# The last spreading of a decoder layer: identity products around the last down product, and the sampled tile in four quarters of the partitions

## The chip, the cores and the metric

One NeuronCore of a Trainium2 chip runs the whole kernel in one launch. The metric is the device time in microseconds, here the median of a few plain executions. A further execution is recorded by the hardware profiler; every row below comes from it. Engines that matter here: TensorE (matmul, PE in the rows, its weight loads PEld), VectorE (DVE), ScalarE (ACT), GpSimd (POOL) and SyncE (SP), which issues most of the transfers.

## The reference, cut to what matters

A decoder layer for 512 prompt tokens and 32 sampled tokens (8 sequences of 4), rows of 1024 float32. The change concerns only the last lines: the weighted outputs of the experts are added to the residual rows, and the result goes through a final RMS norm.

```
y = jnp.zeros((n, D_MODEL), jnp.float32)
for e in range(N_EXPERTS):
    h = jax.nn.silu(xt @ w_gate[e]) * (xt @ w_up[e])
    y = y + combine[:, e:e + 1] * (h @ w_down[e]).astype(jnp.float32)
...
xp = xp + _hier_moe(...)
xs = xs + _hier_moe(...)
y_prompt = _rms(xp, final_norm_g)
y_sample = _rms(xs, final_norm_g)

def _rms(x, g):
    y = xf * lax.rsqrt(jnp.mean(xf * xf, axis=-1, keepdims=True) + EPS)
    return (y * g.astype(jnp.float32)).astype(x.dtype)
```

## The kernel before, in words

The order of the work is written out by hand in the source, engine by engine; semaphores connect them. The 544 tokens lie in five tiles of rows: tiles 0 to 3 of 128 prompt tokens, and tile 4 (`PT`) of the 32 sampled ones.

The 16 experts are worked off in a row of turns. A turn gathers the tokens of an expert, transposes them, multiplies by the gate and up weights (`first_of`), and after the product of the two the down weights (`last_of`). The output rows, scaled by their weights (`y_out`: half the columns by ScalarE, half by VectorE), are added to the residual rows in DRAM (`scratch_x3`) by an indirect DMA of GpSimd. So it goes for the first 14 turns. The last two (`E - 2` and `E - 1`, 64 places each) leave their 64 + 64 output rows in the tile `y_last` instead (it lies in `tabs`). TensorE then spreads them over the tokens: `rows_of_last` (in `cst`) holds for each of the 128 rows a one in the column of its token, and a product of it with `y_last` gives for a tile of tokens what the last two experts add. The sums of a tile lie in the PSUM banks `SUM_BANK[i] + n`, tile i and column half n.

For the light last expert the hidden rows are first transposed (`light_turned`, line 1295, `ps<-cst,qT`), copied by VectorE (L2569) and then multiplied with the down weights (`light_down`, `ps<-ring,qT 64x512`, the weights in four pieces with a semaphore each, `wd_last0` to `wd_last3`).

Meanwhile SyncE loads the residual rows back from `scratch_x3` into `x2` (in `xr`) once all adds have landed (`y_all`), tile 0 first. It issues them on the same queue as the weights. Tile 4 waits besides for the product that still reads this place.

How a tile gets its sum differs. For tiles 0, 1 and 4 the product goes to PSUM and VectorE adds it to `x2` (`summed`). For tiles 2 and 3 TensorE does the adding: an identity product (`ident` with `x2`, `ps<-xr,cst` in the rows) opens the accumulation and the spreading product closes it. Then ScalarE squares and sums a tile's rows and takes the root (`square_and_root`), VectorE takes the reciprocal and multiplies by it and by the weights of the norm (`last_norm`, `gf`), and SyncE stores. The order of the spreading is `SPREAD`, that of the norms `NORM_ORDER` (0, 1, 2, 4, 3). All this stands in one side of a branch on `more`, which is zero here; the other side serves overflowing experts.

Of the kernel before, what the change touches and what calls it, by code (L numbers as in the profile page):

```python
# [21 lines left out]
ALU = mybir.AluOpType  # L22
ACT = mybir.ActivationFunctionType
AX = mybir.AxisListType.X
# [153 lines left out]
def hybrid_layer(nc, t, o):  # L178
# [5 lines left out]
    with ExitStack() as ctx:  # L184
# [156 lines left out]
        SPREAD = ((0, 0), (0, 1), (1, 0), (1, 1), (4, 0), (4, 1), (2, 0), (2, 1), (3, 0), (3, 1))  # L341
# [4 lines left out]
        gf = [buf[:, PT * W:TILES * W] for buf in (ugr, vnr)]  # L346
        y_last = tabs[:, 1024:2048]
# [117 lines left out]
        def _(sp):  # L465
# [206 lines left out]
            for i in range(TILES):  # L672
                if i == PT:
                    sp.wait_ge(sem("y_mm"), 2 * E - 2)
                load(x2[0:ROWS[i], i, :], scratch_x3[i * P:i * P + ROWS[i], :], "x3_in%d" % min(i, 3))
            for i in NORM_ORDER[0:TILES - 1]:
                sp.wait_ge(sem("out_ready"), NORMED[i] + 1)
                dst = o[0][i * P:(i + 1) * P, :] if i < PT else o[1]
                sp.dma_start(dst, x2[0:ROWS[i], i, :]).then_inc(sem("stored"), 16)
# [4 lines left out]
            sp.wait_ge(sem("stored"), 16 * (TILES + 1))  # L684
# [3 lines left out]
        def _(te):  # L688
# [771 lines left out]
            def last_expert_spread(i, n):  # L1460

                j = SUMMED[i][n] - 1
                te.wait_ge(sem("last_rows"), 2)
                te.wait_ge(sem("y_out%d" % n), E)
                bank = pb[SUM_BANK[i] + n]
                if i == PT:
                    te.wait_ge(sem("x3_summed"), SUMMED[0][n])
                    for q in (2 * n, 2 * n + 1):
                        ins = mm(bank[NS * (q % 2):NS * (q % 2) + NS, 0:256], rows_of_last[:, SEQ:TOK],
                                 y_last[:, 256 * q:256 * q + 256])  # L1470
                elif i in (2, 3):
                    te.wait_ge(sem("x3_in%d" % i), 16 if i < 3 else 32)
                    mm(bank, ident, x2[:, i, W * n:W * n + W], True, False)
                    ins = mm(bank, rows_of_last[:, P * i:P * i + P], y_last[:, W * n:W * n + W], False, True)
                else:
                    ins = mm(bank, rows_of_last[:, P * i:P * i + P], y_last[:, W * n:W * n + W])
                ins.then_inc(sem("spread_mm"), 1)

            def last_experts_spread():

                for i, n in SPREAD:
                    last_expert_spread(i, n)

            with te.If(more == 0):
                last_experts_spread()
            with te.Else():
                te.wait_ge(sem("y_out0"), E)
# [11 lines left out]
                last_experts_spread()  # L1499
# [3 lines left out]
        def _(act):  # L1503
# [369 lines left out]
            def squares_and_roots():  # L1873
# [3 lines left out]
                def square_and_root(i):  # L1877
                    if i in (2, 3):
                        act.wait_ge(sem("spread_mm"), SUMMED[i][1])
                        A(ring[:, 2 + i // 4, D * (i % 4):D * (i % 4) + D].rearrange("p (n w) -> p n w", n=2),  # L1880
                          ps[:, SUM_BANK[i]:SUM_BANK[i] + 2, :], ACT.Square,
                          accum_out=small[:, 2 * i:2 * i + 1]).then_inc(sem("x3_sq"), 1)
                    else:
                        act.wait_ge(sem("x3_summed"), SUMMED[i][1] if i < 2 else 6)
                        A(ring[0:ROWS[i], 2 + i // 4, D * (i % 4):D * (i % 4) + D], x2[0:ROWS[i], i, :], ACT.Square,
                          accum_out=small[0:ROWS[i], 2 * i:2 * i + 1]).then_inc(sem("x3_sq"), 1)
                    act.wait_ge(sem("x3_sq"), NORMED[i] + 1)
                    A(small[:, 32 + i:33 + i], small[:, 2 * i:2 * i + 1], ACT.Sqrt, bias=small[:, 16:17], scale=1.0 / D
                      ).then_inc(sem("rstd"), 1)

                for i in NORM_ORDER:
                    square_and_root(i)
# [13 lines left out]
        def _(dve):  # L1906
# [732 lines left out]
            def summed(i, n):  # L2639

                j = SUMMED[i][n]
                if n == 0:
                    dve.wait_ge(sem("x3_in%d" % min(i, 3)), 16 if i < 3 else 32)
                dve.wait_ge(sem("spread_mm"), j)
                bank = pb[SUM_BANK[i] + n]
                if i == PT:
                    for q in (2 * n, 2 * n + 1):
                        v = x2[0:NS, PT, 256 * q:256 * q + 256]
                        ins = V.tensor_tensor(v, bank[NS * (q % 2):NS * (q % 2) + NS, 0:256], v, ALU.add)
# [5 lines left out]
            def last_norm(i):  # L2655
                rows = ROWS[i]
                dve.wait_ge(sem("rstd"), 5 + TILES + NORMED[i])
                rs = small[0:rows, 32 + i:33 + i]
                link(V.reciprocal(small[:, 32 + i:33 + i], small[:, 32 + i:33 + i]))
                if i in (2, 3):  # L2660
                    for n in range(2):
                        ins = V.scalar_tensor_tensor(out=x2[:, i, W * n:W * n + W], in0=pb[SUM_BANK[i] + n], scalar=rs,
                                                     in1=gf[n], op0=ALU.mult, op1=ALU.mult)
                        if i == 3 or n == 1:
                            ins.then_inc(sem("out_ready"), 1)
                else:
                    for n in range(2):
                        v = x2[0:rows, i, W * n:W * n + W]
                        ins = V.scalar_tensor_tensor(out=v, in0=v, scalar=rs, in1=gf[n][0:rows, :],
# [3 lines left out]
            def sums_and_norms():  # L2673
# [3 lines left out]
                link(V.memset(small[:, 16:17], EPS))  # L2677
                summed(0, 0)
# [5 lines left out]
                summed(4, 1)  # L2684
# [230 lines left out]
```

## Time and profile before

| what | us |
|---|---|
| median of 3 plain executions | 715.03 (714.4 to 716.43) |
| profiled execution, its own time | 718.91 |
| its span in the trace | 717.2 |
| TensorE busy | 663.7 (93% of the span) |
| the last 17.4 us: from the first spreading product to the end | 699.8 to 717.2 |

Times in the rows are microseconds from the span's start, unless marked ns. A line number is that of the kernel before; L690 is the helper of nearly all products, so a product is told by its tiles: `ps<-tabs,cst` is a spreading product, `ps<-xr,cst` an identity product, `ps<-ring,qT` a down product. A float32 product is two passes on TensorE, so 16 instructions are 8 products. Instructions of one kind that follow each other are merged in a row with their count. The order lists below are of the program, not of an execution, and hold no times.

### The profile page before, as it was taken

Reading aid. Unit: us, or ns where it says so; the run is one execution under the profiler, and the core shown is the slowest. Engines: PE = TensorE matmul, PEld = TensorE weight load, DVE = VectorE, ACT = ScalarE, POOL = GpSimd, SP = SyncE. Lnnn points to the kernel's source line nnn. Section 1 sums busy time; section 2 is a strip of 40 time slices with the busy share of each in tenths; the row PEclk is TensorE's granted clock in tenths of the full one; section 3 lists DMA queues with packets and bytes.
Section 4 is the critical chain, followed back from the end, with each engine's and each line's share of the span. In section 5 each row is a group of like instructions: output and inputs, shape, how many; then the busy total and the mean of one; then the engine's idle time right before and its main releaser. Section 6 shows DMA issues by size and latency. Waiting matters only on the chain.

```text
span 717.2 us, 14789 instructions
## 1 busy us (share of the span) xinstructions
PE 663.7 (93%) x5458; PEld 427.2 (60%) x5458; DVE 260.9 (36%) x817; ACT 184.2 (26%) x460; POOL 143.8 (20%) x227
## 2 busy tenths in 40 slices
PE   4999998999998888989999977999999999889796
PEld 2486597847646356557555555865685856455342
DVE  4147210137435656765234582112111011111116
ACT  3110213112132883576332211011111010101104
POOL 0405017130143086500000202011211111110000
PEclk9999999999999999999999977999999999999999
DMA  9996138153479075602497258999999999999973
GB/s 336 377 341 210 49 134 291 45 191 118 149 236 358 31 219 154 215 1 83 158 429 301 83 177 291 405 382 392 377 372 408 370 384 386 372 390 390 357 256 131
DMA packets 56785, 185.60 MB, mean 259 GB/s; under 512 B 9021, under 2 KB 30814, under 8 KB 50562
## 3 DMA queue, kind: packets, MB, share of 16 engines
q1 hardware_dynamic: 44914, 152.54, 56.2%
q0 software_dynamic: 11792, 32.05, 14.6%
q8 instruction: 45, 0.74, 0.4%
q14 instruction: 34, 0.28, 0.1%
HBM read 172.57 MB, written 13.93 MB: 260 GB/s over the span
## 4 chain that ended last, share of the span: by engine, by line
PE 75%; DMA 10%; DVE 6%; SPq 4%; ACT 2%; issue 2%; DVEq 0%; POOLq 0%; ACTq 0%
PE ps L690 69%; DMA ring<-in_w_down_dram 6%; SPq L467 3%; PE ps L939 2%; DMA ring<-in_cmp_pages_dram 1%; PE ps L1209 1%; DMA ring<-in_w_in_dram 1%; SPq L427 1%; DMA h_rows<-tabs 1%; PE ps L786 1%; PE ps L966 1%; ACT tabs L1650 1%; DMA ugr<-h_rows,qbd 1%; DVE vnr L2200 0%; DVE xr L2196 0%
## 5 line engine op out<-in xcount | busy, mean ns | idle before, releaser
L690 PE MATMUL ps<-ring,xr 128*128 128x512 f32 (+3 forms) x640 | 140.0, 415 | 9.6 <-DMA ring<-in_w_in_dram 9.6
L690 PEld LDWEIGHTS ps<-ring,xr 128*128 128x128 f32 (+1 forms) x640 | 68.8, 152 | 72.9 <-issue 59.8
L690 PE MATMUL ps<-ring,vnr 128*32 128x128 f32 (+1 forms) x1152 | 78.9, 326 | 2.8 <-DMA ring<-in_w_gate_dram 2.3
L690 PE MATMUL ps<-ring,work 128*32 128x128 f32 (+2 forms) x512 | 70.7, 368 | 0.5 <-DVE xr L2317 0.5
L690 PEld LDWEIGHTS ps<-ring,vnr 128*32 128x32 f32 (+1 forms) x1152 | 54.9, 124 | 27.0 <-issue 10.9
L427 POOL DMA_DIRECT2D ring<-in_sel_pages_dram x96 | 51.6, 537 | 92.1 <-issue 57.1
L690 PE MATMUL ps<-ring 128*128 128x128 f32 (+1 forms) x512 | 60.2, 279 | 1.9 <-DMA ring<-in_cmp_pages_dram 1.9
L2821 POOL DMA_INDIRECT x_rows<-kvn,qbd x14 | 20.5, 1466 | 199.9 <-DVE kvn L2589 58.4
L690 PEld LDWEIGHTS ps<-ring 128*128 128x128 f32 x512 | 59.1, 191 | 2.4 <-DMA ring<-in_cmp_pages_dram 2.1
L2539 DVE COPY vnr<-ps 128x256 f32<-128x256 f32 (+3 forms) x16 | 8.1, 508 | 143.7 <-PE ps L1209 143.7
L690 PE MATMUL ps<-ring,qT 128*32 128x256 f32 (+2 forms) x320 | 52.8, 490 | 5.2 <-DMA ring<-in_w_down_dram 4.5
L427 POOL DMA_DIRECT2D ring<-in_cmp_pages_dram x64 | 34.8, 544 | 81.1 <-PE ps L690 54.3
L690 PEld LDWEIGHTS ps<-ring,work 128*32 128x32 f32 (+1 forms) x512 | 33.9, 130 | 28.4 <-issue 27.1
L1650 ACT ACTIVATE tabs<-tabs,rt 128x128 f32<-128x128 f32 (+3 forms) x64 | 35.4, 559 | 18.6 <-DVE rt L2053 18.6
L690 PEld LDWEIGHTS ps<-ring,qT 128*32 128x32 f32 (+2 forms) x320 | 19.9, 128 | 31.8 <-issue 28.0
L2053 DVE CUSTOM_DVE_ANT_0 tabs<-ps,tabs 128x128 f32<-128x128 f32 (+3 forms) x64 | 28.0, 487 | 14.7 <-PE ps L690 13.9
L1813 ACT COPY vnr<-ps 128x256 f32<-128x256 f32 (+3 forms) x16 | 7.0, 440 | 86.3 <-PE ps L1209 86.3
L939 PEld LDWEIGHTS ps<-cst,tabs 128*128 128x128 f32 x160 | 17.7, 144 | 12.1 <-issue 7.2
L939 PE MATMUL ps<-cst,tabs 128*128 128x128 f32 x160 | 22.7, 284 | 1.8 <-ACT xr L1660 0.9
L690 PE MATMUL ps<-xr,kvn 128*64 128x128 f32 (+2 forms) x264 | 22.9, 310 | 0.3 <-DVE xr L2156 0.3
L690 PE MATMUL ps<-vnr,ring 128*128 128x128 f32 x192 | 21.8, 275 | 0.0
L690 PEld LDWEIGHTS ps<-vnr,ring 128*128 128x128 f32 x192 | 21.6, 192 | 0.0
(401 smaller groups left out, 819.9 us busy)
## 6 DMA issues: line engine op xcount, KB each, us to landing
ring<-in_w_gate_dram SPq DMA_DIRECT2D x11, 2048.0 KB, 26.1
ring<-in_w_down_dram SPq DMA_DIRECT2D x10, 2048.0 KB, 33.5
ring<-in_w_up_dram SPq DMA_DIRECT2D x9, 2048.0 KB, 27.4
xr<-in_w_gate_dram SPq DMA_DIRECT2D x5, 2048.0 KB, 32.6
tabs<-in_w_up_dram SPq DMA_DIRECT2D x5, 2048.0 KB, 35.5
ring<-in_cmp_pages_dram SPq DMA_DIRECT2D x64, 128.0 KB, 5.1
ring<-in_cmp_pages_dram POOLq DMA_DIRECT2D x64, 128.0 KB, 5.3
ring<-in_w_in_dram SPq DMA_DIRECT2D x3, 2048.0 KB, 9.0
```

The costliest lines, as they stand in the source:

```text
L427: eng.dma_start(dst[:, 256 * j + part.start:256 * j + part.stop], table[bass.ds(page, 1), :, part].rearrange("o p n -> (o p) n")).then_inc ...
L467: sp.dma_start(dst, src).then_inc(sem(name), 16)
L690: return nc.tensor.matmul(out, lhsT, rhs, start=start, stop=stop)
L786: ins = nc.tensor.transpose(bank[:, 128 * m:128 * m + rows], src, ident[0:rows, 0:rows])
L939: ins = nc.tensor.transpose(pb[4 + g][:, at:at + P], prob[s % 3][:, g, n * k + P * m:n * k + P * m + P], ident)
L966: ins = nc.tensor.transpose(pb[7][:, P * h:P * h + P], oT[pair % 2][:, P * h:P * h + P], ident)
L1209: ins = nc.tensor.transpose(pb[k // 4][:, P * (k % 4):P * (k % 4) + cap], xe[par][0:cap, P * k:P * k + P], ident[0:cap, 0:cap])
L1650: A(v, v, ACT.Exp, scale=-1.0, bias=rt[:, 160 + u % 32:161 + u % 32], accum_out=rt[:, total:total + 1]).then_inc(sem("probs"), 1)
L1813: nc.scalar.copy(xeT[par][:, 0:4, 0:cap], pb[0][:, :].rearrange("p (k n) -> p k n", k=4)[:, :, 0:cap]).then_inc(sem("xt_ready"), 1)
L2053: return V.tensor_tensor_reduce(out, a, b, scale, 3.0e38, ALU.add, ALU.min, acc)
L2539: V.tensor_copy(xeT[par][:, 4:8, 0:cap], pb[1][:, :].rearrange("p (k n) -> p k n", k=4)[:, :, 0:cap]).then_inc(sem("xt_ready"), 1)
L2821: po.indirect_dma_start(scratch_x3, bass.IndirectOffsetOnAxis(slot_tokens[0:cap, n:n + 1].bitcast(U32), 0), ye[n % 2][0:cap, :], None, com ...
```

## The change

Four things change, all behind the last gate and up products.

TensorE: the branch on `more` is taken before the last expert's transposes. On the usual side the identity product of tile 2's first half (`own_rows(2, 0)`) stands between the transposes and the last down product, that of its second half (`own_rows(2, 1)`) behind the down product, ahead of the scaled copies. The two spreading products of tile 2 then stand alone.

The rows of tile 2 are the first that SyncE loads.

The sampled tile lies in four quarters of the partitions: 256 of its 1024 columns on each 32 partitions (`pt_quarters`), and the norm's weights in the same way (`gf_quarters`). SyncE loads and stores it in four pieces and the norm's weights in four more. One group of four products fills it, one VectorE instruction sums it, one norms it. ScalarE squares it before tile 2.

Each row's squares are then spread over four partitions. VectorE builds a matrix with ones where two partitions hold the same token (`same_row`), and TensorE multiplies it with the partial sums (128x1, `ps<-small,xr`), between the two halves of tile 3. ScalarE takes that root from PSUM.

On TensorE, at the end of the last gate and up products and around the last down product (`ps<-ring,qT`), before:

```order
L690 MATMUL ps<-ring,vnr 64x256 x7
L1295 MATMUL ps<-cst,qT 128x128 [waits y_out1,y_out0,hl_ready]
L1295 MATMUL ps<-cst,qT 128x128
L1457 TENSOR_LOAD ints
L1457 ISA x2
L690 MATMUL ps<-ring,qT 64x512 [waits y_out1,wd_last0,y_out0,h_ready]
L690 MATMUL ps<-ring,qT 64x512
L690 MATMUL ps<-ring,qT 64x512 [waits wd_last1]
```

And now:

```order
L701 MATMUL ps<-ring,vnr 64x256 x7
L1467 TENSOR_LOAD ints
L1467 ISA x2
L1504 COMPARE_AND_BRANCH
L1306 MATMUL ps<-cst,qT 128x128 [waits y_out1,y_out0,hl_ready]
L1306 MATMUL ps<-cst,qT 128x128
L701 MATMUL ps<-xr,cst 128x512 [waits y_out0,x3_in2]
L701 MATMUL ps<-ring,qT 64x512 [waits y_out1,wd_last0,y_out0,h_ready]
L701 MATMUL ps<-ring,qT 64x512
L701 MATMUL ps<-ring,qT 64x512 [waits wd_last1]
```

The read of the flag and the branch moved ahead of the transposes, and a product that waits for the load of tile 2 (`x3_in2`) stands ahead of the down product. Then the spreading from tile 1's second half on, before:

```order
L690 MATMUL ps<-tabs,cst 128x512 [waits y_out1,last_rows]
L690 MATMUL ps<-tabs,cst 32x256 [waits x3_summed,y_out0,last_rows]
L690 MATMUL ps<-tabs,cst 32x256
L690 MATMUL ps<-tabs,cst 32x256 [waits x3_summed,y_out1,last_rows]
L690 MATMUL ps<-tabs,cst 32x256
L690 MATMUL ps<-xr,cst 128x512 [waits x3_in2,y_out0,last_rows]
L690 MATMUL ps<-tabs,cst 128x512
L690 MATMUL ps<-xr,cst 128x512 [waits x3_in2,y_out1,last_rows]
L690 MATMUL ps<-tabs,cst 128x512
```

And now, to the end of tile 3:

```order
L701 MATMUL ps<-tabs,cst 128x512 [waits y_out1,last_rows]
L701 MATMUL ps<-tabs,cst 32x256 [waits y_out1,x3_summed,y_out0,last_rows]
L701 MATMUL ps<-tabs,cst 32x256 x3
L701 MATMUL ps<-tabs,cst 128x512 [waits y_out0,last_rows]
L701 MATMUL ps<-tabs,cst 128x512 [waits y_out1,last_rows]
L701 MATMUL ps<-xr,cst 128x512 [waits x3_in3,y_out0,last_rows]
L701 MATMUL ps<-tabs,cst 128x512
L701 MATMUL ps<-small,xr 128x1 [waits x3_sq,x3_summed,last_rows]
L701 MATMUL ps<-xr,cst 128x512 [waits x3_in3,y_out1,last_rows]
L701 MATMUL ps<-tabs,cst 128x512
```

Tile 2 has lost its identity products here, the four products of the sampled tile stand in one group, and the one-column product is new; it waits for ScalarE's square of the sampled tile.

The diff, cut to its core:

```diff
-        SPREAD = ((0, 0), (0, 1), (1, 0), (1, 1), (4, 0), (4, 1), (2, 0), (2, 1), (3, 0), (3, 1))
+        SPREAD = ((0, 0), (0, 1), (1, 0), (1, 1), (4, 0), (2, 0), (2, 1), (3, 0), (4, 1), (3, 1))
+        pt_quarters = x2[:, PT, 0:256]
+        gf_quarters = x2[:, PT, 256:512]
+        same_row = x2[:, PT, 512:512 + P]
+        SQUARED = (0, 1, PT, 2, 3)
...
-            for i in range(TILES):
-                if i == PT:
-                    sp.wait_ge(sem("y_mm"), 2 * E - 2)
-                load(x2[0:ROWS[i], i, :], scratch_x3[i * P:i * P + ROWS[i], :], "x3_in%d" % min(i, 3))
+            for i in (2, 0, 1, 3):
+                load(x2[:, i, :], scratch_x3[i * P:i * P + P, :], "x3_in%d" % i)
+            sp.wait_ge(sem("y_mm"), 2 * E - 2)
+            for q in range(4):
+                at = slice(256 * q, 256 * q + 256)
+                load(pt_quarters[NS * q:NS * q + NS, :], scratch_x3[SEQ:TOK, at], "vectors_in")
+                load(gf_quarters[NS * q:NS * q + NS, :], t["gf"][:, at].to_broadcast([NS, 256]), "vectors_in")
...
+                if i == PT:
+                    for q in range(4):
+                        sp.dma_start(o[1][:, 256 * q:256 * q + 256], pt_quarters[NS * q:NS * q + NS, :]).then_inc(sem("stored"), 16)
...
-            light_turned(E - 1)
             more = te.value_load(ints[0:1, 80:81], min_val=0, max_val=1)
-            last_of(E - 1)
+            def own_rows(i, n):
+                te.wait_ge(sem("x3_in%d" % i), 16)
+                te.wait_ge(sem("y_out%d" % n), E - 1)
+                mm(pb[SUM_BANK[i] + n], ident, x2[:, i, W * n:W * n + W], True, False)
...
+                if i == PT and n == 1:
+                    te.wait_ge(sem("x3_summed"), 5)
+                    te.wait_ge(sem("x3_sq"), SQUARED.index(PT) + 1)
+                    mm(pb[SUM_BANK[0] + 1][:, 0:1], same_row, small[:, 2 * PT:2 * PT + 1]).then_inc(sem("spread_mm"), 1)
+                    return
...
             with te.If(more == 0):
-                last_experts_spread()
+                light_turned(E - 1)
+                own_rows(2, 0)
+                last_of(E - 1)
+                own_rows(2, 1)
+                last_experts_spread(2)
...
+                elif i == PT:
+                    V.scalar_tensor_tensor(out=pt_quarters, in0=pt_quarters, scalar=rs, in1=gf_quarters,
+                                           op0=ALU.mult, op1=ALU.mult).then_inc(sem("out_ready"), 1)
...
+                link(V.tensor_reduce(four_units, ident.rearrange("p (q m) -> p m q", q=4), AX, ALU.add))
+                link(V.tensor_copy(same_row.rearrange("p (q m) -> p q m", q=4), four_units[:, None, :].to_broadcast([P, 4, NS])))
```

## Rows read from the trace of the kernel before

**Rows 1.** The chain that ended last, from 671 us: start, us, what.

```profile
681.48 12.28 PE ps L690 x80
...
694.26 0.45 PE ps L1295 x2
...
694.73 0.43 DVE qT L2569
...
699.01 0.67 ACT tabs L1853
...
699.82 11.74 PE ps L690 x32
...
711.58 1.12 ACT ring L1880 x2
...
712.73 0.31 ACT small L1888
...
713.06 0.17 DVE small L2659
...
713.93 0.74 DVE xr L2662
```

**Rows 2.** Line L683, the last two stores: issue to landing.

```profile
DMA to landing us min/median/max: 2.1/2.1/2.2
```

**Rows 3.** Timeline of PE, 671 to 700: start, us; in brackets idle before.

```profile
673.62 5.52 PE L690 MATMUL ps<-ring,qT 128*64 128x512 f32 x48 [2.09 <-DMA ring<-in_w_down_dram]
...
681.48 2.71 PE L690 MATMUL ps<-work,qT 128*64 128x512 f32 x8 [1.97 <-DVE qT L2569]
...
695.34 3.65 PE L690 MATMUL ps<-ring,qT 128*64 128x512 f32 x16 [0.64 <-DVE qT L2569]
```

**Rows 4.** Timeline of SyncE: the last weight piece, then the five residual loads.

```profile
672.37 0.91 SPq L467 DMA_DIRECT2D ring<-in_w_down_dram  x1
...
690.54 3.02 SPq L467 DMA_DIRECT2D xr<-x_rows  x5
```

**Rows 5.** DMA issues from 672.35 and from 690.5, landing last; then spacing (ns).

```profile
ring<-in_w_down_dram SPq DMA_DIRECT2D x1, 512.0 KB, 23.2
...
xr<-x_rows SPq DMA_DIRECT2D x1, 512.0 KB, 6.3
...
L467 SPq DMA_DIRECT2D xr<-x_rows x5: 338/424/1211, 690.5 to 693.1; - x5
```

**Rows 6.** Stretches: length, PE busy (instructions), granted clock, DMA share, GB/s.

```profile
672.00:676.00 4.00, 2.38 (x12) 1.00 1.02 402
679.10:682.50 3.40, 1.43 (x12) 1.00 0.76 319
682.50:685.90 3.40, 3.40 (x12) 0.50 0.74 278
693.80:695.30 1.50, 0.44 (x2) 1.00 1.05 421
```

**Rows 7.** Timeline of the tail, 699 to 707, VectorE and TensorE.

```profile
701.06 1.45 DVE L2652 TENSOR_TENSOR xr<-ps,xr 128x512 f32<-128x512 f32 x2 [1.11 <-PE ps L690]
...
703.42 0.58 PEld L690 LDWEIGHTS ps<-tabs,cst 128*32 128x32 f32 x8 [0.76 <-issue]
...
704.17 0.84 DVE L2649 TENSOR_TENSOR xr<-ps,xr 32x256 f32<-32x256 f32 x2
...
704.41 1.13 PE L690 MATMUL ps<-xr,cst 128*128 128x512 f32 x2
...
705.38 1.02 PE L690 MATMUL ps<-tabs,cst 128*128 128x512 f32 x2
...
706.23 1.02 PE L690 MATMUL ps<-xr,cst 128*128 128x512 f32 x2
```

**Rows 8.** Groups by shape: count, busy us, mean ns, idle before.

```profile
L690 PE MATMUL ps<-ring,qT 128*32 128x256 f32 x160 | 9.7, 382 | 0.0
L690 PE MATMUL ps<-small,ugr 128*128 128x1 f32 x8 | 0.9, 240 | 0.0
```

More of the change, by code:

```diff
@@ L1463, in last_expert_spread @@
                 te.wait_ge(sem("last_rows"), 2)
-                te.wait_ge(sem("y_out%d" % n), E)
+                if i == PT and n == 1:
[3 more added lines that the diff above has]
+                    return
+                for half in range(2):
+                    if i == PT or n == half:
+                        te.wait_ge(sem("y_out%d" % half), E)
@@ L1882, in square_and_root, with root @@
                           accum_out=small[:, 2 * i:2 * i + 1]).then_inc(sem("x3_sq"), 1)
-                    else:
[L1884 to L1892, printed above, removed]
+                    elif i == PT:
+                        act.wait_ge(sem("x3_summed"), 5)
+                        A(ring[:, 3, 0:256], pt_quarters, ACT.Square, accum_out=small[:, 2 * i:2 * i + 1]
+                          ).then_inc(sem("x3_sq"), 1)
+                    else:
+                        act.wait_ge(sem("x3_summed"), SUMMED[i][1])
+                        A(ring[:, 2, D * i:D * i + D], x2[:, i, :], ACT.Square,
+                          accum_out=small[:, 2 * i:2 * i + 1]).then_inc(sem("x3_sq"), 1)
+                def root(i):
+                    act.wait_ge(sem("x3_sq"), SQUARED.index(i) + 1)
+                    if i == PT:
+                        act.wait_ge(sem("spread_mm"), SUMMED[PT][1])
+                    A(small[:, 32 + i:33 + i], pb[SUM_BANK[0] + 1][:, 0:1] if i == PT else small[:, 2 * i:2 * i + 1], ACT.Sqrt,
+                      bias=small[:, 16:17], scale=1.0 / D).then_inc(sem("rstd"), 1)
+                square(0)
+                root(0)
+                square(1)
+                root(1)
+                square(PT)
+                square(2)
+                root(2)
+                root(PT)
+                square(3)
+                root(3)
             with act.If(more == 0):
@@ L2655, in last_norm @@
             def last_norm(i):
-                rows = ROWS[i]
                 dve.wait_ge(sem("rstd"), 5 + TILES + NORMED[i])
-                rs = small[0:rows, 32 + i:33 + i]
+                rs = small[:, 32 + i:33 + i]
                 link(V.reciprocal(small[:, 32 + i:33 + i], small[:, 32 + i:33 + i]))
@@ L2683, in sums_and_norms @@
                 last_norm(0)
-                summed(4, 1)
                 last_norm(1)
```

48 lines of the change are left out of this document (25 added, 23 removed).

## The prediction

> **What bounds the kernel now.** I read the last 45 us backwards, since the change touches nothing earlier. First the chain of waits in order of time [rows 1]. The last stretch has three parts. TensorE runs expert by expert (to 693.76), then a short relay with VectorE for the last expert: transposes at 694.26, copy of the hidden rows at 694.73, down product at 695.34. Then come the scaled copies (699.01) and, without a hole, 11.74 us of spreading products (699.82 to 711.56). What follows is a fixed relay for tile 3: ScalarE's square 1.12 us, root 0.31, VectorE's reciprocal 0.17, two normalizing passes (713.26 to 714.67), and the last store, which lands 2.1 us after its issue [rows 2]. So in the tail TensorE is the bound, and each microsecond of product taken from it is worth one, as long as VectorE, ScalarE and the stores keep up.
>
> Second, TensorE's own idle time and its releasers [rows 3]: 0.64 us before the last down product, and 0.5 us before the transposes (694.26 less 693.76 [rows 1]). These are the holes that the change wants to fill. Third, the loads on SyncE's queue: when they are issued [rows 4] and how long after that they land [rows 5], and the stretches with their granted clock [rows 6]. They say when the data is there that a filled hole needs.
>
> **The sum in the tail (behind the scaled copies).**
> 1. The identity products of tile 2, (2,0) and (2,1), leave the tail. A 128x512 float32 product is two passes, and in the tail one starts 0.86 us after the other (705.38 to 706.23; the first after a change of shape takes 0.96, 704.41 to 705.38 [rows 7]). Two identity products: 2 x 0.86 = 1.72 us saved.
> 2. The four 32-row products of the sampled tile now stand on four column quarters at once. Before they took from 703.42 to 704.41, 0.99 us, two at a time [rows 7]. Four at a time the trace has elsewhere: 160 passes of 128*32 by 256 columns in 9.7 us, 0.061 us a pass [rows 8]. Eight passes are 0.49 us. Saved: 0.4 to 0.5 us; I take 0.4.
> 3. The new one-column product that adds up the quarters' squares: eight passes of 128x1 took 0.9 us [rows 8], so two passes 0.22 us, up to 0.35 if the change of shape costs 0.1. It costs 0.25.
> Sum: 1.72 + 0.4 - 0.25 = 1.87 us less TensorE in the tail.
>
> Does something take its place? Call T the start of the first spreading product. The tiny product waits for ScalarE's square of the quarters. VectorE's sums of tiles 0 and 1 end by 704.17 [rows 7], T+4.4; the single 128x256 sum takes 0.42 (half of the 0.84 row), so T+4.8. ScalarE is then inside tile 1's square and root, 1.5 us behind 704.2 by the rows of tile 3 (1.12 + 0.31 [rows 1]), so to T+5.9, and squares a quarter of the columns in at most half of the 1.12 us: T+6.5. TensorE reaches the tiny product at T+7.5: it doesn't wait. VectorE: with the second pair of 32-row sums (0.84) gone it goes by the roots: root 2 at T+8.0 (TensorE is done with tile 2 at T+6, ScalarE free at T+6.5, square and root 1.45), tile 2 normalized at T+9.6, the sampled tile at T+10.3. Root 3 arrives at T+9.87+1.47 = T+11.3. Free. SyncE issues four quarter stores instead of one, 0.4 us apart as its loads are [rows 5]: from T+10.5 to T+12.1, and the first half of tile 3 wants it at T+12.3. Close (0.2 us), but hidden. The new reduction and copy on VectorE (two small passes, 0.3 us each) run while it waits for the first spreading product (it ends 1.2 us behind T, and VectorE's first sum starts at 701.06 [rows 7]): nothing. The eight small loads take 8 x 0.4 us of SyncE after 693.1, and are wanted at T+4.4: nothing. The second identity product, (2,1), stands between the down product and the copies, in the hole between the down product's end at 698.99 and 699.82 [rows 1, 3], 0.83 us: 0 to 0.1.
>
> **The sum in front of it (the step that decides).** The first identity product (2,0) is put between the transposes and the last down product. TensorE works in order, so whatever the product waits for, the down product waits for too. It waits for the load of tile 2 to land. The load is issued at 690.54, when all adds into the residual rows have landed (POOL's signal, unchanged), and tile 2 is now the first load. The first load of before lands 6.3 us later, at 696.8 [rows 4, 5]. It is so late because the queue is full: the last piece of the down weights, issued at 672.37, lands 23.2 us later, at 695.6 [rows 4, 5]; the DMAs move 421 GB/s there [rows 6], 512 KB take 1.25 us, and 695.6 + 1.25 is 696.8. Changing which tile is first doesn't move that point. TensorE is ready at 694.7. It will stand 2.1 us, then do 0.86 to 0.96 us of product (the first after a change of shape: 0.96), and start the last down product at 696.87 + 0.96 = 697.8 instead of 695.34: +2.5 us. All of T moves with it. The value read and the branch, now ahead of the transposes, are hidden in the stand.
>
> Net on the profiled execution: +2.5 - 1.87 = +0.6 us, from a span of 717.2 to 717.8.
>
> The clock. A stand of TensorE of 1.97 us before 681.48 was followed by half clock, 0.50, that is 1.2 GHz, from 682.5 to 685.9; a stand of 2.09 us before 673.62 was not (672 to 676 at 1.00) [rows 3, 6]. The new stand of 2.1 us, with 0.44 us of transposes in the 1.5 us before it, is of that kind, so half clock may follow: 3.4 us of it, of which 2.7 us would be product time, cost half of that, 1.4 us. Bounds: 0 and 1.7. I take 0.7.
> The Trainium skill (TensorE: Matmul & The Clock Gate, "HAM oscillation — how this bites in real kernels") says that a matmul stream that stands waiting for a DMA comes back throttled and pays half of the throttled time. The trace agrees in one of the two stands above.
> On the landing itself, the Trainium skill (DMA: Bandwidth & Descriptors, "Why a DMA increments its semaphore by 16 and not by 1") says that a load counts as landed only when each of its engines is done, so the slowest engine sets the wait. Where the wait would be shorter is a landing counted by its first engines; the rule speaks against that, and with the 6.3 us row, which is such a full count, the stand stays 2.1 us.
>
> Likeliest: +0.6 + 0.7 = +1.3 us. The profiled execution took 718.91 us with a span of 717.2; the three plain runs have a median of 715.03, 3.9 us less, and spread over 2.0. I add the difference to the median: 716.3 us. Its own range: +0.6 to +2.0, 715.6 to 717.0.
>
> **Rivals.**
> A. The load is there in time. Without the profiler the queue may be ahead: 2.1 us earlier is enough. Then the product starts at 694.8, ends at 695.75, and the down product is 0.4 us late (0.6 with the value read and branch in front of the transposes: the read took 0 extra before, being inside the copy). Net 0.5 - 1.87 = -1.4 us, 713.6. For it: plain runs are 3.9 us shorter, and something in them is faster. Against: TensorE itself was released at 673.6 by the same kind of late weight load [rows 3], so a faster queue brings TensorE forward too, and the distance between them stays.
> B. The stand is longer. In executions where half clock doesn't follow the stand at 681.48 (it cost 1.7 us, half of 3.4 us [rows 6]), TensorE comes to the product at 693.1 and stands 3.8 us, while the landing is where it was. Before is then 1.7 us shorter and after is not: +0.6 + 1.7 = +2.3 us, and with half clock behind the new stand up to +3.7. Time 717.3 to 718.7. It decides once TensorE stands about 3.6 us. For it: the same length of stand did not lower the clock at 673.6. Against: in the one profile it did at 681.48.
> C. The tail isn't cut. If the quarter stores, the tiny product's wait or the last root hold tile 3 back, at most 1.87 us of the gain go. With half of it gone the sum is +2.2 us, 717.3. For it: 0.2 us of slack at the stores. Against: all other slacks are 0.9 us or more.
>
> **Chances.** A measurement of this kernel tells about 0.3%, 2.1 us, from no change. Forecast 0.47 (0.43 within, 0.04 slower, by its upper end and the clock), A 0.26 (0.17 within, 0.09 faster, since a landing far ahead of need and run differences of 1 us would take it there), B 0.21 (0.02 within, 0.19 slower), C 0.06 (half slower). Faster 0.09, within 0.65, slower 0.26. Range: from A with 0.3 us to spare, 713.3, to B with half clock, 718.7.
>
> **What would show it.** In the new profile: an idle of TensorE of about 2 us before the product that reads the residual rows ahead of the last down product, released by the load, which lands at about 696.8; the down product starting at about 697.8 and still 3.65 us long (longer means half clock). From the first spreading product to TensorE's end 9.9 us instead of 11.74. The sampled tile's four products within 0.5 us. No idle of TensorE before the one-column product; VectorE waiting for the last root. A load that has landed before 694.8 makes the forecast wrong and A right; a spreading stretch above 11 us makes the sum in the tail wrong.

## The result, and the profile after

The changed kernel takes 723.06 us (median of 17 runs, 719.3 to 727.42), the kernel before 718.28 beside it (17 runs, 713.62 to 723.24). The two medians are 4.8 us apart. The ratio on record, which is not that of the medians, is 1.0082, with an interval of 1.006 to 1.0103: 5.9 us slower (4.3 to 7.4). The prediction was 716.3 us, 1.3 us slower and so within 0.3% of before. It was wrong in the time, in the range (713.3 to 718.7) and in the likeliest outcome: slower by more than 0.3% had a chance of 0.26.

The profiled execution took 723.93 us with a span of 722.2, against 717.2: 5.0 us more. I read it as the prediction did, from the stand of TensorE on. First TensorE's timeline (start, us, instructions; idle before and its releaser in brackets), which answers to [rows 3, 7]:

```profile
681.37 1.94 PE L701 MATMUL ps<-work,qT 128*64 128x512 f32 x8 [1.97 <-DVE qT L2613]
...
690.75 1.95 PE L701 MATMUL ps<-ring,vnr 128*64 128x256 f32 x16 [0.54 <-DMA ring<-in_w_up_dram]
693.22 0.44 PE L1306 MATMUL ps<-cst,qT 128*128 128x128 f32 x2 [0.53 <-DVE qT L2597]
697.06 2.07 PE L701 MATMUL ps<-xr,cst 128*128 128x512 f32 x2 [3.40 <-DMA xr<-x_rows]
699.06 5.74 PE L701 MATMUL ps<-ring,qT 128*64 128x512 f32 x16
704.73 1.12 PE L701 MATMUL ps<-xr,cst 128*128 128x512 f32 x2
705.69 6.12 PE L701 MATMUL ps<-tabs,cst 128*128 128x512 f32 x20
...
713.37 0.28 PE L701 MATMUL ps<-small,xr 128*128 128x1 f32 x2
...
714.45 1.02 PE L701 MATMUL ps<-tabs,cst 128*128 128x512 f32 x2
```

The identity product stands 3.40 us for the load of tile 2. It then takes 2.00 us to the next start where one took 0.96 [rows 7], and the down product 5.67 where it took 3.65 [rows 3]. The first spreading product starts at 705.69, 5.87 us later than at 699.82 [rows 1]. From there to TensorE's end it is 9.78 us (714.45 + 1.02 - 705.69) instead of 11.74: the tail was cut as forecast, and the one-column product waits for nothing.

The stretches with their granted clock (length, PE busy, clock, DMA share, GB/s), which answer to [rows 6]:

```profile
682.50:685.90 3.40, 3.40 (x22) 1.00 0.76 282
...
692.70:696.10 3.40, 0.44 (x2) 1.00 1.02 401
696.10:699.50 3.40, 2.44 (x4) 0.55 0.72 233
699.50:702.90 3.40, 3.40 (x10) 0.50 0.06 21
702.90:706.30 3.40, 3.40 (x12) 0.94 0.00 0
```

Two things moved. The half clock (0.50, that is 1.2 GHz) of 682.5 to 685.9 [rows 6] is absent here, though the stand of 1.97 us ahead of it is the same. So TensorE came to the end of the last transposes at 693.66 instead of 694.70, although it now also waited 0.54 us for weights. And behind the new stand the clock was halved over about 6.8 us: from late in the stand, through the identity product and the whole down product.

The chain of waits (start, us, what), which answers to [rows 1]:

```profile
681.65 8.75 DMA x_rows<-kvn,qbd
...
690.46 6.55 DMA xr<-x_rows
...
697.06 18.43 PE ps L701 x50
...
717.85 0.74 DVE xr L2705
```

The chain no longer runs through TensorE's expert products ahead of 693.76 [rows 1]. It comes from the last adds into DRAM (landed at 690.40) and the load behind them, 6.55 us (6.3 before [rows 5]). TensorE's earlier coming is lost in the stand.

Last the stores: SyncE's timeline, then the last two stores alone (duration, landing), which answer to [rows 4, 2].

```profile
690.46 2.98 SPq L472 DMA_DIRECT2D xr<-x_rows  x5
...
712.01 3.38 SPq L690 DMA_DIRECT2D out_dram<-xr  x3
715.64 1.96 SPq L688 DMA_DIRECT2D out_dram<-xr  x4
717.96 1.55 SPq L694 DMA_DIRECT2D out_dram<-xr  x2
```

```profile
L694 SPq DMA_DIRECT2D out_dram<-xr x2: 350/622/893, 718.0 to 718.6; - x2
...
DMA to landing us min/median/max: 2.7/3.0/3.2
```

The quarter stores are done at 717.60, before the last tile's halves are ready: their spacing is hidden, as forecast. But the very last store takes 0.89 us to issue and lands 3.2 us after its start, against 2.1 [rows 2]. In the kernel before the same two stores take 0.99 us together:

```profile
714.04 0.99 SPq L683 DMA_DIRECT2D out_dram<-xr  x2
```

While these stores are issued, the DMA engines also carry transfers that the page calls `instruction`. The queues (packets, MB, share of 16 engines), now from 717.9 to 719.6:

```profile
q1 hardware_dynamic: 198, 0.30, 50.7%
q8 instruction: 1, 0.02, 4.1%
q14 instruction: 1, 0.01, 1.3%
```

And before, from 713.9 to 715.1:

```profile
q1 hardware_dynamic: 71, 0.14, 39.7%
q14 instruction: 1, 0.01, 2.8%
```

The one packet of q8, 16 KB, is new at this place. (Both traces hold 45 of q8 in all, and the last of before runs from 709.09 to 710.05, between two stores.) It runs from 718.03 to 719.14, and the last store's issue (718.62 to 719.51) ends 0.38 us behind it.

The sum on the profiled executions: +5.87 in front, -1.96 in the tail, +1.09 from TensorE's end to the end (722.2 less 715.47 is 6.73; 717.2 less 711.56 is 5.64). That is +5.0. All of the 1.09 lies behind the start of the last store, 0.56 of it in its issue.

### The profile page after: what moved, and what is told of

Read it like the earlier page. It is cut to its first block, busy times and chain, and to the rows that moved or that the text cites. A ratio compares the mean times of both kernels' runs of the same rounds, so it can differ in the third digit from the quotient of the medians.

```text
span 722.2 us, 14807 instructions
## 1 busy us (share of the span) xinstructions
PE 665.3 (92%) x5460; PEld 426.0 (59%) x5460; DVE 259.4 (36%) x815; ACT 182.7 (25%) x460; POOL 143.5 (20%) x227
## 4 chain that ended last, share of the span: by engine, by line
PE 67%; DMA 16%; SPq 6%; DVE 6%; issue 2%; ACT 2%; POOL 0%; POOLq 0%; DVEq 0%; ACTq 0%
PE ps L701 61%; DMA ring<-in_w_down_dram 6%; SPq L472 5%; DMA x_rows<-kvn,qbd 3%; DMA ugr<-h_rows,qbd 2%; PE ps L950 2%; SPq L432 1%; DMA ring<-in_w_in_dram 1%; DMA ring<-in_cmp_pages_dram 1%; PE ps L1220 1%; DMA h_rows<-tabs 1%; DMA xr<-x_rows 1%; PE ps L797 1%; PE ps L977 1%; ACT tabs L1676 1%
## 5 line engine op out<-in xcount | busy, mean ns | idle before, releaser
L701 PE MATMUL ps<-ring,qT 128*32 128x256 f32 (+2 forms) x320 | 56.6, 516 | 6.3 <-DMA ring<-in_w_down_dram 6.3
```

The source lines that it names most:

```text
L701: return nc.tensor.matmul(out, lhsT, rhs, start=start, stop=stop)
```

## The experiments

An execution of this program comes to its last stretch several us earlier or later than another, for reasons far ahead of the change (e5 and e6 below come about 4 us late). So besides the ratio I read three distances in each profile: F, from the end of the last transposes to the first spreading product; S, from there to TensorE's end; E, from there to the span's end. The end of the transposes is their start plus 0.44, TensorE's end the last product's start plus 1.02. Before: F 5.12, S 11.74, E 5.64.

| kernel | F | S | E | sum, less before's 22.50 | timed ratio (interval), us |
|---|---|---|---|---|---|
| after | 12.03 | 9.78 | 6.73 | +6.0 | 1.0082 (1.006 to 1.0103), +5.9 |
| e1 | 5.92 | 9.73 | 6.42 | -0.4 | 0.9986 (0.9955 to 1.0016), -1.0 |
| e2 | 11.13 | 10.86 | 5.61 | +5.1 | 1.0034 (1.0005 to 1.0063), +2.4 |
| e3 | 5.13 | 11.72 | 5.85 | +0.2 | 0.9998 (0.9962 to 1.0035), -0.1 |
| e4 | 8.77 | 9.78 | 6.60 | +2.7 | 1.0043 (1.0009 to 1.0076), +3.1 |
| e5 | 5.12 | 11.53 | 6.17 | +0.3 | 0.9994 (0.9963 to 1.0025), -0.4 |
| e6 | 5.03 | 11.72 | 5.58 | -0.2 | 0.9978 (0.994 to 1.0016), -1.6 |
| e7 | 5.93 | 9.73 | 14.73 | +7.9 | 1.0144 (1.0095 to 1.0194), +10.3 |
| e8 | 5.92 | 9.74 | 7.68 | +0.8 | 1.0007 (0.9975 to 1.0039), +0.5 |
| e9 | 6.88 | 9.77 | 6.69 | +0.8 | 1.0056 (1.0025 to 1.0087), +4.0 |
| e10 | 5.06 | 10.83 | 5.73 | -0.9 | 0.9987 (0.9955 to 1.002), -0.9 |
| e11 | 5.92 | 9.74 | 7.72 | +0.9 | 1.0015 (0.9983 to 1.0047), +1.1 |

The last column turns the ratio into us by the median of before in the same set. The two columns agree within the intervals but for e2 and e9. Both have a stand, and two things about a stand differ from execution to execution.

The first is its length. In the 12 profiles in which SyncE issues it, the first residual load lands 5.3 (e3) to 8.2 us (e8) after its issue. Counted from the end of the last transposes, the first load of all 13 profiles lands 0.5 (e5) to 3.7 us (e7, e8) later, 2.1 in before, 3.4 in the changed kernel, 2.8 at the median of the 13. It was never there in time.

The second is the half clock behind it. A timed run has its mean granted clock on record, over the whole execution. 6.8 us at half clock take 0.0047 from such a mean (half of 6.8 in 720). The averages over the runs are 0.9799 for the kernel before (in each of three sets), 0.9756 for the changed kernel, 0.9795 for e1, 0.9782 for e2, 0.9786 for e4, 0.9769 for e9 and 0.9805 for e10, with errors of 0.0006 to 0.0017. By an estimate from these the changed kernel has about 6 us more of half clock than before, and e1 and e10 next to none. For e2 it is 2.6 us, less than the 6.8 of its profile, and for e9 4.3 us, where the profile has none behind the stand. Other stretches of half clock are in these means too (the longer end alone adds up to 1 us in the changed kernel and e9), so this is a sign and not a proof.

**e1: the product behind the last down product.** The changed kernel with one line moved.

```diff
-                own_rows(2, 0)
                 last_of(E - 1)
+                own_rows(2, 0)
                 own_rows(2, 1)
```

> The changed kernel with one move: both identity products of tile 2 stand behind the last down product, none ahead of it. Theory S (the stand): the 3.4 us stand for the load of tile 2 and the half clock behind it are the whole loss. Then both go, the down product starts as early as in the kernel before and takes 3.65 us, the second identity product sticks out of the 0.83 us hole by about 0.9 us, the tail keeps its saving of 1.96 us, and the late last store (1.1 us) stays: within 1 us of the kernel before, and about 5 us faster than the changed kernel. Rival R (the rest): the loss comes from the quarters, the branch or the new order of the loads; then it stays 3 us or more slower than before.

TensorE's timeline:

```profile
694.14 3.65 PE L701 MATMUL ps<-ring,qT 128*64 128x512 f32 x16 [0.52 <-DVE qT L2613]
697.73 1.98 PE L701 MATMUL ps<-xr,cst 128*128 128x512 f32 x4
699.55 6.08 PE L701 MATMUL ps<-tabs,cst 128*128 128x512 f32 x20
...
708.26 1.02 PE L701 MATMUL ps<-tabs,cst 128*128 128x512 f32 x2
```

The stand is gone, the down product takes 3.65 us again, and the slowdown with it: from 1.0082 to 0.9986, intervals that don't touch. So the place of this one product is the cause of the loss. The tail keeps its 2.0 us, yet only 0.4 us of them reach the end: two products (1.82 us) don't fit the hole of 0.83 us behind the down product (F +0.80), and the last store keeps its delay (E +0.78).

**e2: the stand alone.** The kernel before, with tile 2 loaded first, the branch moved ahead, and only (2,0) ahead of the down product.

```diff
-            for i in range(TILES):
+            for i in (2, 0, 1, 3, 4):
...
-                last_experts_spread()
+                light_turned(E - 1)
+                own_rows(2, 0)
+                last_of(E - 1)
+                last_experts_spread((2, 0))
```

> The kernel before with one part of the change: tile 2 is loaded first, the branch is taken ahead of the transposes, and the identity product (2,0) stands ahead of the last down product; the sampled tile and all else as before. Theory S: the full loss of the front part is here, +5.9 us in front and 0.9 us back in the tail, so +4 to +5.5 us against before, with a stand of 2 to 4 us for the load and half clock behind it. Rival R: within 1 us of before.

TensorE's timeline, then the stretches with their clock:

```profile
696.01 2.07 PE L690 MATMUL ps<-xr,cst 128*128 128x512 f32 x2 [2.81 <-DMA xr<-x_rows]
698.01 5.46 PE L690 MATMUL ps<-ring,qT 128*64 128x512 f32 x16
704.33 5.71 PE L690 MATMUL ps<-tabs,cst 128*128 128x512 f32 x18 [0.86 <-ACT tabs L1862]
```

```profile
694.00:696.00 2.00, 0.00 (x0) 0.71 1.04 420
696.00:698.00 2.00, 1.99 (x2) 0.50 0.38 104
```

The stand and the half clock come back without any of the quarters: they belong to the product's place. The profile shows F +6.0, and less of the tail to pay it with. The timed runs say +2.4 us (0.4 to 4.5), less than expected and less than the profile. The clock fell inside the stand: 0.71 over a stretch in which TensorE did nothing. I take it that it doesn't fall in each execution. The timed runs' mean clock, 0.0018 below before's where the full half clock would take 0.0047, speaks for that, but doesn't show it run by run.

**e3: the order of the loads alone.** The kernel before with `for i in (2, 0, 1, 3, 4)`.

> The kernel before with only the order of the residual loads changed to tiles 2, 0, 1, 3, 4. Theory S: the first load lands about 6.5 us after its issue whichever tile it is, tile 0 lands at about 699 and is wanted at 701: no difference, within 0.5 us. Rival: tile 0 comes late for VectorE's first sum and the tail starts later, +0.5 us or more.

Nothing changes in F or S, and the ratio is 0.9998. The first load, now tile 2's, lands 5.3 us after its issue (6.3 in before), the second, tile 0's, 6.2. So the new order delays nothing. That it brings the first load forward isn't shown either, for that landing scatters from 5.3 to 8.2 us.

**e4: the stand filled.** The changed kernel with three products ahead of the identity product that nobody reads. They keep TensorE busy while it waits.

```diff
+                te.wait_ge(sem("last_rows"), 2)
+                for _ in range(3):
+                    mm(pb[0], ident, rows_of_last[:, 0:W])
                 own_rows(2, 0)
```

> The changed kernel with three more 128x512 float32 products between the transposes and the identity product (2,0), 2.6 us of TensorE into a free bank; the result isn't used. They fill most of the stand and change nothing that is waited for. Theory S with the clock as a part of its own: the load lands at the same time, no half clock follows, the identity product takes 0.96 us in place of 2.0 and the down product 3.65 in place of 5.7, so 2.5 to 3.1 us faster than the changed kernel and 2.5 to 3 us slower than before. Rival (the stand alone is the loss, half clock is chance): no faster than the changed kernel.

TensorE's timeline, and the stretches at the end of the stand and behind it:

```profile
697.48 2.74 PE L701 MATMUL ps<-cst 128*128 128x512 f32 x6
700.82 1.12 PE L701 MATMUL ps<-xr,cst 128*128 128x512 f32 x2 [0.60 <-DMA xr<-x_rows]
701.88 3.65 PE L701 MATMUL ps<-ring,qT 128*64 128x512 f32 x16
...
706.42 6.12 PE L701 MATMUL ps<-tabs,cst 128*128 128x512 f32 x20
```

```profile
700.00:702.00 2.00, 1.40 (x5) 1.00 0.88 228
702.00:704.00 2.00, 2.00 (x10) 1.00 0.18 69
```

The wait for the load is as long (from 697.65 to 700.82, 3.17 us), but the clock stays at 1.00 and the down product at 3.65. From the product's start to the first spreading it is 5.60 us, against 8.63 in the changed kernel (697.06 to 705.69). So in the profiles the half clock costs 3.0 us and the wait costs the rest. Work that nobody needs wins about half of the loss back: F + S + E is 3.4 us shorter than in the changed kernel, and the timed runs say +3.1 us instead of +5.9. Their intervals overlap (0.6 to 5.5 and 4.3 to 7.4), so the timing alone doesn't separate the two.

**e5: the quarters alone.** The changed kernel with the order of loads and of TensorE's front as before; the four identity products of tiles 2 and 3 stand in the tail.

```diff
-            for i in (2, 0, 1, 3):
+            for i in (0, 1, 2, 3):
...
-                own_rows(2, 0)
-                last_of(E - 1)
-                own_rows(2, 1)
-                last_experts_spread(2)
+                last_experts_spread(None)
```

> The changed kernel with TensorE's front as in the kernel before: no identity product outside the spreading, branch and value read where they were, residual loads in the order 0, 1, 2, 3. What is left of the change is the sampled tile in four quarters. Theory: TensorE's spreading gets 0.2 to 0.3 us shorter (0.4 to 0.5 less for the four products at once, 0.25 more for the one-column product), and the last store, issued behind four more stores, lands 3 us after its issue in place of 2.1: +0.5 to +1 us against before. Rival: the quarters cost nothing at the end of the program and it is 0.2 us faster or the same.

TensorE's first spreading products, and SyncE's last two stores:

```profile
703.40 4.24 PE L701 MATMUL ps<-tabs,cst 128*128 128x512 f32 x16 [0.83 <-ACT tabs L1875]
```

```profile
717.42 1.30 SPq L694 DMA_DIRECT2D out_dram<-xr  x2
```

S is 0.21 us shorter (the prediction's 0.4 less 0.25). The last store pays more than that back: the two take 1.30 us instead of 0.99, and E is 0.53 longer. The quarters by themselves bring nothing.

**e6: the branch alone ahead of the transposes**, in the kernel before.

```diff
-            light_turned(E - 1)
             more = te.value_load(ints[0:1, 80:81], min_val=0, max_val=1)
-            last_of(E - 1)
...
             with te.If(more == 0):
+                light_turned(E - 1)
+                last_of(E - 1)
                 last_experts_spread()
```

> The kernel before with the value read and the branch ahead of the last expert's transposes, nothing else. Theory: the read takes 0.5 us of TensorE's queue while it waits for VectorE's hidden rows anyway, so the transposes start at most 0.2 us later and the down product 0 to 0.2 us earlier behind them: within 0.3 us of before. Rival: the branch refetches instructions and holds the transposes 1 us or more.

The idle before the down product falls from 0.64 to 0.52 us (0.52 in e1 and e10 too), since the read of the flag no longer stands there: 0.1 us in F, and nothing that the timing can tell (0.9978).

**e7: the quarter stores issued by GpSimd**, with e1's order. It asks whether four stores on SyncE's queue hold the last one back.

```diff
-            for i in NORM_ORDER[0:TILES - 1]:
+            for i in NORM_ORDER[0:TILES - 2]:
...
+            po.wait_ge(sem("out_ready"), NORMED[PT] + 1)
+            for q in range(4):
+                po.dma_start(o[1][:, 256 * q:256 * q + 256], pt_quarters[NS * q:NS * q + NS, :]).then_inc(sem("stored_quarters"), 16)
```

> Both identity products of tile 2 behind the down product (as in the first experiment), and the four quarter stores issued by GpSimd in place of SyncE. Theory: the late last store (issue of 1.0 us and landing 2.9 us after it starts) comes from the four stores ahead of it on SyncE's queue; without them it is issued in 0.33 us and lands after 2.1: 0.7 to 1.1 us faster than the first experiment, 1.5 to 2.5 us faster than before. Rival: the DMAs themselves are slow with the 1 KB rows, or GpSimd's stores land last: no faster than the first experiment.

GpSimd's stores and SyncE's last two:

```profile
712.51 2.11 POOL L2895 DMA_DIRECT2D out_dram<-xr  x4 [26.98 <-DVE xr L2706]
...
714.56 1.86 SPq L690 DMA_DIRECT2D out_dram<-xr  x2
```

SyncE's last two stores still take 1.86 us together. So it isn't the quarter stores on its queue that slow the last issue. And the kernel became 10.3 us slower by something else: TensorE ends at 712.07, yet the span ends at 726.8. The trace holds a drain of GpSimd at the end of its program, from 717.57 to 726.54, 8.97 us. In the other twelve profiles the same drain takes 8.65 us and starts between 691.6 and 699.2, beside other work, since nothing late is left for GpSimd to issue.

**e8: one store for the quarters**, with e1's order.

```diff
-                    for q in range(4):
-                        sp.dma_start(o[1][:, 256 * q:256 * q + 256], pt_quarters[NS * q:NS * q + NS, :]).then_inc(sem("stored"), 16)
+                    sp.dma_start(o[1].rearrange("r (q c) -> q r c", q=4), pt_quarters).then_inc(sem("stored"), 64)
```

> As the first experiment, with the sampled tile stored by one transfer of 128 rows of 1 KB (four-quarter pattern on the DRAM side) in place of four of 32 rows. Theory as for the one with GpSimd's stores, if the number of stores on SyncE's queue is what counts: 0.7 to 1.1 us faster than the first experiment. Rival: the transfer is shared by fewer DMA engines and lands later than the last store: 0 to 1 us slower than the one with GpSimd's stores.

The issue of the very last store falls to 0.67 us, but E is 7.68, 1.3 us longer than in e1. What grew is the way from issue to landing: the last packet of that store ends 3.6 us after the start of the issue, against 2.4 in e1. One store instead of four isn't better.

**e9: tile 2's first half on ScalarE's queue**, 256 KB, in the changed kernel. If the load is late because it queues behind the weights on SyncE's queue, its own queue should bring it in time; if the DMA engines themselves are behind, it should not.

```diff
-                load(x2[:, i, :], scratch_x3[i * P:i * P + P, :], "x3_in%d" % i)
+                at = slice(W if i == 2 else 0, D)
+                load(x2[:, i, at], scratch_x3[i * P:i * P + P, at], "x3_in%d" % i)
...
+                act.dma_start(x2[:, 2, 0:W], scratch_x3[2 * P:3 * P, 0:W]).then_inc(sem("x3_first"), 16)
```

> The changed kernel, identity product (2,0) ahead of the down product as changed, but the half tile that it reads (256 KB) is loaded on ScalarE's queue, issued by ScalarE at the same signal, about 690.5, instead of behind the weights on SyncE's queue. Theory Q (the landing is late because the load stands behind the down weights in the same queue): it lands 3 to 4 us after its issue, TensorE stands under 1 us, no half clock: 4 to 6.5 us faster than the changed kernel, 0 to 1.5 us faster than before. Rival (the DMA engines themselves are full, or the adds' signal is what is late): it lands 6 us or more after its issue and the kernel is as slow as the changed one.

The load in the chain of waits, then TensorE's timeline:

```profile
690.27 5.72 DMA xr<-x_rows
```

```profile
696.03 1.13 PE L702 MATMUL ps<-xr,cst 128*128 128x512 f32 x2 [1.27 <-DMA xr<-x_rows]
697.09 3.65 PE L702 MATMUL ps<-ring,qT 128*64 128x512 f32 x16
...
701.64 6.12 PE L702 MATMUL ps<-tabs,cst 128*128 128x512 f32 x20
```

Theory Q wanted 3 to 4 us, and it is 5.72 for half the bytes, with the DMA share at 1.02 and 415 GB/s (694 to 696). So its own queue doesn't bring it in time, and the busy DMA engines are the likelier reason. Whether the queue gains anything isn't shown: whole tiles on SyncE's queue landed after 5.3 to 8.2 us, and this load differs in size as well as in queue. TensorE came late here (transposes end at 694.76), stood 1.27 us, and the clock did not fall: from the product to the spreading it is 5.61 us, as in e4. The profile's sum is +0.8, the timed runs say +4.0 us (1.8 to 6.2). The timed runs' mean clock is 0.0030 below before's, as if about half of them had the 6.8 us of half clock that the profiled one lacks. Which ones isn't known, so this difference stays open.

**e10: one identity product in the hole behind the down product**, in the kernel before, without quarters. It is e2 with `own_rows(2, 0)` behind `last_of(E - 1)`.

> The kernel before with the branch ahead, tile 2 loaded first and one identity product, (2,0), behind the down product in the hole before the scaled copies land; sampled tile and stores as before. Theory: the product fits the hole with 0.1 us over and leaves the tail 0.86 us shorter, and nothing is late at the end: 0.7 to 1.0 us faster than before, at the limit of what the timing tells. Rival: the product in the hole delays the first spreading product by as much as it saves.

TensorE's timeline, and SyncE's last two stores:

```profile
695.20 3.65 PE L690 MATMUL ps<-ring,qT 128*64 128x512 f32 x16 [0.52 <-DVE qT L2578]
698.78 1.13 PE L690 MATMUL ps<-xr,cst 128*128 128x512 f32 x2
699.74 5.68 PE L690 MATMUL ps<-tabs,cst 128*128 128x512 f32 x18
```

```profile
713.06 1.00 SPq L683 DMA_DIRECT2D out_dram<-xr  x2
```

This is the part of the idea that costs nothing: one product (0.96 us to the next start) fills the hole of 0.83, F stays at 5.06, S is 0.91 shorter, E is nearly as before. The profile says -0.9 us, the timing 0.9987 (0.9955 to 1.002), which can't be told from no change.

**e11: three transfers instead of twelve** for the sampled tile and the norm's weights (one load each, one store), with e1's order.

```diff
+            sp.dma_start(pt_quarters, scratch_x3[SEQ:TOK, :].rearrange("r (q c) -> q r c", q=4)).then_inc(sem("vectors_in"), 64)
+            sp.dma_start(gf_quarters, t["gf"].rearrange("o (q c) -> q o c", q=4).to_broadcast([4, NS, 256])).then_inc(sem("vectors_in"), 64)
```

> Both identity products behind the down product, and the quarters moved by 3 transfers in place of 12: one load of the rows, one of the norm's weights, one store. Theory: what delays the last store is the number of transfers on the queue; it is then issued in 0.33 us and lands 2.1 us later: 0.7 to 1.1 us faster than the first experiment. Rival: the last store still takes 2.6 us or more from issue to landing, since each of these transfers runs on few DMA engines.

The last store's issue still takes 0.64 us, and E is 7.72 as in e8, again with 3.7 us from the issue to the last packet. Fewer transfers don't mend the end.

## Why the prediction was wrong

- **The tail: right.** 1.87 us forecast, 1.96 measured. Its parts hold too: one identity product less is 0.91 in e10 (forecast 0.86), the quarters with the one-column product 0.21 in e5 (forecast 0.15). Nothing on ScalarE or VectorE takes their place.
- **The wait of the first identity product: the mechanism right, the size not.** "It will stand 2.1 us" was 3.40. The load landed 0.2 us from where it was forecast (697.0), with some luck: over the profiles that point scatters by 3 us. TensorE came 1.04 us earlier, mainly since the half clock behind the stand ahead of 681 was absent. This is rival B, which had 3.8 us for it and a chance of 0.21; I held the one profile's half clock against it. Of the 13 profiles 9 have that half clock and 4 (after, e3, e6, e7) don't. B's step fits: where TensorE is early the kernel before is shorter and the changed one is not. But even B's upper end, +3.7 us, is short of the measured difference, since it priced the clock by the same bound. Measured from the transposes the loss is 6.0 us, by the two spans 5.0; the timed ratio says 5.9, the medians 4.8. e1 (stand gone, loss gone) and e2 (stand alone, loss there) show the cause.
- **The clock: the step that failed.** "I take 0.7, bounds 0 and 1.7." It cost 3.0 us (8.63 less 5.60 in e4, 5.61 in e9). The bound was read from the one stretch of half clock in the last 45 us of the trace of before, 3.4 us [rows 6], as if that were its greatest length. Here the clock was at 0.50 for about 6.8 us, and these covered the two products on the path. The same trace of before already spoke against the bound, further ahead, with 17.1 us at 0.50 and TensorE busy for 8.85 of them (length, PE busy, clock, DMA share, GB/s):

```profile
423.10:440.20 17.10, 8.85 (x43) 0.50 0.68 242
```

The Trainium skill (TensorE: Matmul & The Clock Gate, "HAM oscillation — how this bites in real kernels") has the penalty as half of the throttled time. An estimate by it for 6.8 us is 3.4, with some of the 6.8 inside the stand, and the measured 3.0 agrees. The rule spoke for the loss, and I had weighed it at a half.
- **The last store: missed.** E was forecast unchanged (2.1 us of landing) and is 1.09 longer. Rival C saw danger at the stores, but in the spacing of the quarter stores, which is hidden. What is late is first the issue of the very last one: 0.89 us, and 1.0 to 1.15 in e1, e4 and e9, against 0.33 to 0.34 in before and e10 and 0.44 in e3. It comes with the quarters (e5), also when their stores are on another queue (e7) or few (e8, e11). The traces point to what it waits for, though no run tests it. In all eight profiles with the quarters a 16 KB `instruction` transfer on q8 is under way when that issue starts, and the issue ends 0.35 to 0.38 us after it. In the five profiles without the quarters there is none at that place. In the kernel before the same happens once far ahead: a load issued at 106.55 takes 1.29 us and ends 0.37 us after such a transfer. Why one stands there with the quarters was not found, nor why the store lands another 0.5 us later in the changed kernel.
- **The second identity product in the hole: "0 to 0.1" was right.** From the start of the down product to the first spreading product it is 4.48 us in before (699.82 less 695.34) and 4.54 in e10 and e4, where the clock is at 1.00 in both products: 0.06 us. Two of them cost 0.8 (e1).
- **The load: "changing which tile is first doesn't move that point" held within the scatter** (e3: 5.3 us after the issue, where twelve profiles have 5.3 to 8.2). That a full queue is the reason is neither shown nor refuted: with half the bytes on ScalarE's queue it is 5.7 us (e9). Rival A wanted it there in time, and in none of the 13 profiles was it.
- **The time itself.** I added the difference to 715.03, the median of three runs. With 17 runs it is 718.28, with a spread of 9.6 us, so 3.2 us of the miss of 6.8 lie in the base. The other 3.5 are the difference of the medians, 4.8, less the forecast 1.3, and follow from the steps above.

The three large errors go one way: stand and product +0.35 on the spans, clock +2.3, last store +1.1, tail -0.1, together +3.7 on the forecast +1.3. What stays open: why an `instruction` transfer stands at the last store with the quarters, in how many executions half clock follows a stand (e2 and e9 differ between profile and timing by 3 us, in opposite directions), and whether e10's 0.9 us is real.

## What to carry to other kernels

A product pulled forward into a hole takes its wait with it: ask when its operand lands, not only when the engine is idle, and put it behind the last product that others wait for (e1), as many as the hole holds (e10). Even there look at the landing: in e7 and e8 it came only about 0.4 us before the product. Price a new stand with the clock behind it, over all the product time that follows in the path, and look for the longest stretch of half clock in the whole trace before you call one a bound. Where the engine comes first in every profile, as here, its earlier arrival is worth nothing: the early executions are cut off at the landing. Read arrival and landing in several profiles, since here both scatter by microseconds.

## What the runs showed of the hardware

- The same stand of 1.96 to 1.97 us ahead of the product that starts at 679 to 686 was followed by 3.4 us at 0.50 in 9 of 13 profiles and not in 4 (after, e3, e6, e7). Stands of 2.81 and 3.40 us (e2, after) were followed by about 6.8 us at 0.50, which began inside the stand. Stands of 1.27 us (e9) and 0.60 us (e4) were followed by none.
- GpSimd's drain at the end of its program takes 8.65 us in twelve profiles and 8.97 in e7. There it starts at 717.57, behind GpSimd's late transfers, and ends 0.2 us before the span does.
- A load of 512 KB on SyncE's queue landed 5.3 to 8.2 us after its issue in twelve profiles. 256 KB on ScalarE's queue landed after 5.72 us, while the DMAs moved 379 to 415 GB/s (692 to 696 in e9).
- The issue of one store on SyncE takes 0.33 us as a rule (0.44 for the last one in e3). In the eight profiles with the quarters the last one took 0.64 to 1.20 us and ended 0.35 to 0.38 us after a 16 KB `instruction` transfer on q8.
